# A two-layer mixture of experts behind a hybrid block: expert weights from the third expert on loaded in pieces of 1 MB in place of 2 MB

## The reference, cut to what matters

```
h = h + hybrid_mixer(rmsnorm_2(h, norm_mix[l]), w_in[l], w_branch_a[l], ...)
h = h + expert_choice_ffn(rmsnorm_2(h, norm_ffn[l]), w_router[l],
                          w_expert_gate[l], w_expert_up[l], w_expert_down[l])

# in expert_choice_ffn, cap = 2 * 256 // 16 = 32
gate, idx = lax.top_k(jnp.swapaxes(aff, 1, 2), cap)
xe = h[bidx, idx]
a = jnp.einsum('becd,edf->becf', xe, w_gate)
u = jnp.einsum('becd,edf->becf', xe, w_up)
ye = jnp.einsum('becf,efd->becd', jax.nn.silu(a) * u, w_down)
return jnp.zeros_like(h).at[bidx, idx].add(gate[..., None].astype(h.dtype) * ye)
```

## Time and profile before

| | us |
|---|---|
| runs | 1815.93, 1816.86, 1821.24 |
| median | 1816.86 |
| the profiled execution | 1824.18 |
| its span | 1822.4 |
| PE busy | 1546.2 (85%) |
| DVE busy | 761.6 (42%) |
| ACT busy | 596.6 (33%) |
| HBM read | 564.18 MB, 310 GB/s over the span |

### The profile page before, as it was taken

One profiled execution on the slowest core, in us unless ns is written; L12 is line 12 of the kernel. 1 busy time (PEld: TensorE's weight loads), 2 busy tenths in 40 slices (PEclk: granted clock), 3 DMA queues, 4 the chain that ended last, 5 costly groups with the idle time before them and its releaser, 6 DMA issues.

```text
span 1822.4 us, 34068 instructions
## 1 busy us (share of the span) xinstructions
PE 1546.2 (85%) x15300; PEld 1186.6 (65%) x15300; DVE 761.6 (42%) x1574; ACT 596.6 (33%) x1063; POOL 76.0 (4%) x87
## 2 busy tenths in 40 slices
PE   8999999999999999976666666999999966566665
PEld 7989998999799998533333333799896533233332
DVE  6896668887564665210110110536664201011011
ACT  5765646665455654000000000546642000000001
POOL 1020001000020101000000000001010000000000
PEclk9999999999999999998887877899999987888887
DMA  6443456555473559999999999853489999999997
GB/s 262 175 153 139 147 189 226 190 185 194 165 289 120 206 202 408 413 429 430 430 430 429 430 430 429 344 194 127 195 342 409 428 430 430 430 430 429 429 430 308
DMA packets 45841, 567.44 MB, mean 311 GB/s; under 512 B 6672, under 2 KB 7216, under 8 KB 10496
## 3 DMA queue, kind: packets, MB, share of 16 engines
q1 hardware_dynamic: 40176, 552.62, 73.9%
q0 software_dynamic: 3744, 12.03, 1.8%
q10 hardware_dynamic: 1776, 0.62, 0.1%
HBM read 564.18 MB, written 1.05 MB: 310 GB/s over the span
## 4 chain that ended last, share of the span: by engine, by line
PE 59%; DMA 35%; DVE 3%; another core or an unknown queue 2%; ACT 1%; issue 0%; SPq 0%; DVEq 0%; ACTq 0%
DMA slab<-in_slabs 34%; PE bank L587 14%; PE bank L588 14%; PE bank L589 14%; PE bank L1130 5%; PE bank L1182 2%; PE bank L944 1%; DMA sm<-in_fb 1%; PE bank L1003 1%; PE bank L1200 1%; PE bank L967 1%; PE bank L1107 1%; DVE wl L1222 1%; DVE xc L1345 0%; PE bank L550 0%
## 5 line engine op out<-in xcount | busy, mean ns | idle before, releaser
L1130 PE MATMUL bank<-slab,xe 128*32 128x256 f32 x4096 | 313.5, 462 | 160.2 <-DMA slab<-in_slabs 160.0
L1222 DVE TENSOR_TENSOR wl<-slab,wh 128x1024 fp32r<-128x1024 f32 (+1 forms) x286 | 348.0, 1230 | 186.5 <-ACT wh L1899 186.2
L587 PE MATMUL bank<-hth,wh 128*128 128x256 f32 x1344 | 388.0, 289 | 2.8 <-DVE wl L1222 2.7
L588 PE MATMUL bank<-htl,wh 128*128 128x256 f32 x1344 | 380.7, 283 | 0.0
L589 PE MATMUL bank<-hth,wl 128*128 128x256 f32 x1344 | 380.6, 283 | 0.0
L1899 ACT ACTIVATE wh<-slab 128x1024 fp32r<-128x1024 f32 (+1 forms) x286 | 296.2, 1046 | 169.0 <-PE bank L589 157.8
L1130 PEld LDWEIGHTS bank<-slab,xe 128*32 128x32 f32 x4096 | 142.8, 127 | 310.5 <-DMA slab<-in_slabs 204.2
L587 PEld LDWEIGHTS bank<-hth,wh 128*128 128x128 f32 x1344 | 257.8, 192 | 12.9 <-issue 7.8
L588 PEld LDWEIGHTS bank<-htl,wh 128*128 128x128 f32 x1344 | 257.9, 192 | 0.1
L589 PEld LDWEIGHTS bank<-hth,wl 128*128 128x128 f32 x1344 | 257.7, 192 | 0.0
L1182 PE MATMUL bank<-slab,ha 128*32 128x256 f32 x2048 | 142.7, 427 | 71.3 <-DMA slab<-in_slabs 69.7
(11 more groups left out here) (388 smaller groups left out, 2187.1 us busy)
## 6 DMA issues: line engine op xcount, KB each, us to landing
slab<-in_slabs SPq DMA_DIRECT2D x251, 2048.0 KB, 47.9
slab<-in_slabs SPq DMA_DIRECT2D x23, 1024.0 KB, 10.3
bias<-in_bias POOLq DMA_DIRECT2D x32, 192.0 KB, 3.1
bias<-in_bias POOLq DMA_DIRECT2D x8, 256.0 KB, 5.7
x<-in_x SPq DMA_DIRECT2D x2, 512.0 KB, 4.4
rg<-in_rg POOLq DMA_DIRECT2D x1, 1024.0 KB, 10.5
bt<-in_rel POOLq DMA_DIRECT2D x1, 768.0 KB, 14.6
fg<-in_final_g POOLq DMA_DIRECT2D x1, 512.0 KB, 4.0
```

What stands on the lines that cost most here:

```text
L587: e.matmul(o, wh, xh, start=start, stop=False, skip_group_check=True)
L588: e.matmul(o, wh, xl, start=False, stop=False, skip_group_check=True)
L1130: t = e.matmul(bk[bank][32 * j:32 * j + 32, 0:256], XE[:, c, :], w[:, k, 256 * j:256 * j + 256], start=(c == 0), stop=(c == 7))
L1222: e.tensor_tensor(lo, src, hi.bitcast(F32), ALU.subtract).then_inc(*dve_l.mark(p))
```

## The change

slab_list() names, for experts 3 to 15 of both layers, halves in place of whole slabs. "From the third expert on" counts from zero: experts 0, 1 and 2 keep their pieces. Each half has a load of its own with 1 MB (8 KB for each partition), a semaphore wait of TensorE ahead of its 16 matmuls and a mark behind them, and a slot of its own in slot_plan(). The order of the weights stays. tail_slab becomes the half (1, 0) of eg1_14, as the whole slab is no longer in the list, and the condition on the warming matmuls now names the last down slab of layer 0, so that they stand where they stood.

```diff
@@ slab_list
         for e in range(1, 16):
-            expert(f"eg{l}_{e}", [(0, 1), 1] if e == 2 else [0, 1], "late")
-            expert(f"eu{l}_{e}", [0, 1], "late")
-            expert(f"ed{l}_{e}", [0], "late")
+            both = [(0, 0), (0, 1), (1, 0), (1, 1)]
+            expert(f"eg{l}_{e}", [(0, 1), 1] if e == 2 else both if e > 2 else [0, 1], "late")
+            expert(f"eu{l}_{e}", both if e > 2 else [0, 1], "late")
+            expert(f"ed{l}_{e}", both[0:2] if e > 2 else [0], "late")
             if e == 1:
                 expert(f"eg{l}_2", [(0, 0)], "late")
-            expert(f"ed{l}_{e}", [(1, 0), (1, 1)] if e == 15 else [1], "late")
+            expert(f"ed{l}_{e}", both[2:4] if e > 2 else [1], "late")
@@ build
-    tail_slab = nslab["eg1_14", 1]
+    tail_slab = nslab["eg1_14", (1, 0)]
@@ tensor_program
                     for n, key, k0, nk in parts("ed", l, ex, i):
-                        if l == 0 and type(key) is tuple:
+                        if (l, ex, i) == (0, 15, 1) and type(key) is tuple:
                             warm(2, 5 if key[1] else 2)
```

## The result

| | before, us | changed, us |
|---|---|---|
| median of 9 runs each | 1816.68 | 1823.81 |
| range | 1814.68 to 1822.58 | 1821.98 to 1828.29 |
| ratio, with its 95% interval | | 1.0039 [1.0029, 1.0048] |
| profiled execution (span) | 1824.18 (1822.4) | 1825.38 (1823.5) |

The change costs 7.1 us, 0.39%. The forecast was +10.0 us. It is slower by more than the 0.3% that a measurement of this kernel tells from no change, though the interval reaches down to that.

The account below looks back on a forecast made before the run. The prediction took the expert stages to be bound by DMA, bytes over rate at 430 GB/s. +11.6 us for transfers, 0 for room and release and -1.6 at layer 0's end gave +10.0: 1826.9 us, range 1812.2 to 1833.8.

Parts of the forecast that it names:

- The toll of a transfer: Expert stages: 154 more transfers on the saturated queue, each costing 0.075 us beside its bytes, add 11.6 us.
- F: Cost of a load for being one transfer, beside its bytes; taken as 0.075 us, range 0.03 to 0.11.
- 10 us windows in the mixers: Start of each mixer: 1 MB loads at 421 and 422 GB/s against 429 for 2 MB loads, giving 0.099 us a transfer.
- the two landings at the end: Kernel's very end: two halves landed in 2.41 + 2.43 us against 4.86 for a whole load, giving -0.02 us a transfer.
- The rule that spoke against the change: Skill's 2.0 us fixed per transfer, as a toll +308 us; the prediction held it mostly hidden by other loads in flight.
- Room and release: Expert stages: half-slots, each half asked for once one half two experts earlier is used; a full queue hides it, 0 us.
- rival C of the prediction: Expert stages: the queue of ten transfers runs dry behind 12.8 us issue blocks, 19 us on top, 1846; chance 0.03.
- The end of layer 0: Layer 0's last expert: PE, not the last load, is late; halves start the last up-load's matmuls earlier, -1.6 us.
- The point named ahead as a check: Expert 15's up-load start less expert 9's: 180.3 us by the forecast, 177.6 if the toll is hidden, 174 if engines even out.
- A (hidden): Expert stages: the toll of a transfer is hidden, F from -0.02 to 0.03, 1812.2 to 1819.9 us; chance 0.30.
- B (evened engines): Expert stages: shorter transfers even the 16 engines out, each half landing at 2.42 us, -13.9 us, 1801; chance 0.07.
- D (PE the bound): Expert stages: PE at the low clock becomes the bound, at most +29 us less the DMA's 11.6, near 1845; chance 0.02.

Follow-up runs that it names:

- the two transfers alone: Kernel before with its slots, waits and releases, but each of the 154 slabs issued as two 1 MB transfers: 1823.98 us, ratio 1.0041.
- the second profile of before: The kernel before, unchanged, run and profiled once more: 1817.40 us, ratio 1.0005.
- the run with four transfers: Kernel before, but each of the 154 slabs issued as four 512 KB transfers with 4 KB rows: 1840.83 us, ratio 1.0131.
- the run for the last expert alone: The changed kernel's halves for expert 15 only, both layers; experts 3 to 14 keep 2 MB loads: 1817.58 us, ratio 1.0011 against the kernel before.

## Why the prediction was right, and where it was off

**The bound.** Right. The stages are bytes over rate; the rate fell by 1% and the kernel became 0.39% slower, with what PE, ScalarE and VectorE do nearly unchanged.

**The toll of a transfer, +11.6 us.** Right in its mechanism, and too large by half: the two transfers alone measured 7.7 us, so F is 7.7/154 = 0.050 us, where 0.075 was taken. By the rates it is 2.0972 MB at 426 GB/s less 2.0972 MB at 430, 4.923 - 4.877 = 0.046. The step that was mis-sized is the reading of 10 us windows in the mixers as if they were good to 1 GB/s. The burst of halves itself is the same in every kernel here, but comes at another time in each execution. By the first of its 8 KB packets it is in the changed kernel 3.7 us earlier in layer 0 and 2.5 in layer 1, in the second profile of before 6.0 and 9.5 us earlier. Windows that follow it read 423 and 424 in the changed kernel, and 427 and 418 in the second profile of before, where the first had 421 and 422:

```profile
508.30:518.30 10.00, 10.00 (x86) 10.00 (x85) 8.94 (x8) 5.66 (x8) 3.60 (x2) 1.00 1.00 423
1171.50:1181.50 10.00, 10.00 (x86) 10.00 (x85) 4.90 (x7) 5.98 (x8) 0.00 (x0) 1.00 1.01 424
```
```profile
506.00:516.00 10.00, 10.00 (x85) 10.00 (x85) 8.85 (x8) 6.24 (x8) 3.61 (x2) 1.00 1.01 427
1164.50:1174.50 10.00, 10.00 (x85) 10.00 (x85) 4.91 (x7) 5.90 (x8) 0.00 (x0) 1.00 0.99 418
670.00:680.00 10.00, 10.00 (x85) 10.00 (x85) 6.98 (x8) 3.81 (x5) 0.65 (x1) 1.00 1.02 436
```

(The last line is the window with 2 MB loads, 6 us earlier like the burst: 436, where the first profile had 429.) And in the first profile itself a window 1.0 or 1.5 us later reads 418 in place of 421 and 433 in place of 422:

```profile
513.00:523.00 10.00, 10.00 (x86) 10.00 (x85) 8.79 (x8) 5.47 (x7) 2.63 (x1) 1.00 1.01 418
1175.50:1185.50 10.00, 10.00 (x85) 10.00 (x85) 4.90 (x4) 4.73 (x6) 0.00 (x0) 1.00 1.04 433
```

So such a window is good to 5 or 10 GB/s, and F by the same formula is 0.03 us at 427 GB/s and 0.14 at 418. That the halves are slower than whole loads was read rightly; that the windows agreed within 1 GB/s was chance. The weighing with the two landings at the end, F = -0.02, pulled the term the right way, but that reading is no better: the same three landings of the second profile of before give 2.43 + 2.44 - 4.85 = +0.02. Neither reading alone would have given the time, +15.2 or -3.1 us for the term; the range of F taken around their mean, 0.03 to 0.11, holds the 0.050.

**The rule that spoke against the change.** A further transfer costs 0.014 to 0.017 us beside its rows, though a load lands 27 to 51 us after its issue. The Trainium skill's fixed 2.0 us for a transfer (DMA: Bandwidth & Descriptors, Anatomy of one DMA — SWDGE (gpsimd) path) would have made the change cost 308 us as a toll; the section states it for transfers that GpSimd issues, while the slabs go out on SP. The runs agree with the prediction that it is no toll in a full queue. Rows of 4 KB ran at 419 to 420 GB/s in the stages, and a set of 128 more rows costs 0.036 to 0.040 us. The estimate of 0.078 us, from the 408.7 GB/s that the same page gives for 4 KiB rows (iDMA fabric), is too large here.

**Room and release, 0 us.** Right. Two transfers without them took as long as the change within the intervals (-0.6 us). The queue in flight fell from 51 to 27 us, forecast was 25, and even 12.7 us in the run with four transfers left no dip: rival C of the prediction, the dry queue, has nothing for it, and its condition failed: the longest issue fell with the size of the load, from 12.8 to 6.65 us.

**The end of layer 0, -1.6 us.** Wrong. The step was to take the 12.1 us between the last up-load and the last matmuls for a property of the kernel. It was the clock of one execution (0.50 in both groups; 1.00 in the second in the repetition, and 9.88 us), and the run for the last expert alone shows no gain. What the change was to shorten is in most profiles bounded by the last load in either kernel, and a stretch seen in one profile was put at its full worth in the median. The rest of that step held: the third mixer load's later slot cost nothing, the stretch from the last matmuls of layer 0 to the first of layer 1's experts is 241.46 us where it was 241.45.

**The sum.** +11.6 - 1.6 = +10.0 against +7.7 (transfers alone) and +7.1 (all): the terms were off by -3.9 and by +1.6, and so partly made up for one another, which is luck. The point named ahead as a check, from expert 9's first up-load to expert 15's, is 1131.74 - 953.02 = 178.72 us after, 177.56 before; forecast were 180.3, and 177.6 if hidden. It lies in between, nearer to hidden, but the second profile of before has 1127.26 - 950.59 = 176.67: over 36 loads it was too short a piece to decide, as the steady 426 GB/s did.

**The rivals.** A (hidden) would have been 430 GB/s, B (evened engines) 433, and the forecast 423. The measured 426 refutes A and B, and the two transfers' interval of +5.3 to +9.6 us leaves out A's upper end, F = 0.03, as well. D (PE the bound) is refuted by PE's 67 to 69 us in 100.

## What to carry to other kernels

When a stretch is bound by its transfers, count rows and transfers besides bytes: here two transfers of 8 KB rows in place of one of 16 KB rows cost 0.05 us for each slab of 2 MB, and four of 4 KB rows 0.16, in a queue that was kept full. Finer waits and releases brought nothing here, where 10 loads were in flight. What splitting a last load wins where an engine waits for it, no run here shows; before splitting there look at a second profile, since the clock of one execution moved that place by 2 us, and a small load at the start moved the first expert by 6. Windows of 100 us in a steady stretch agreed within 2 GB/s between the two profiles of before; windows of 10 us read 418 to 433 GB/s for the same burst.

## What wasn't expected of the hardware

Transfers of 64 partitions, one for the lower and one for the upper half, 154 pairs of them, cost 455 us: 228 to 366 GB/s with a DMA share of 1.01, where 128 partitions had 430. The Trainium skill, SBUF — State Buffer, Can I just issue two DMAs to hit both halves?, says that the ports are picked by a single transfer's span of partitions, and that two concurrent transfers, at partition 0 and at partition 64, ran only 6% faster than one. The runs agree that two such halves don't make up one whole transfer: the lowest slice, 228 GB/s, is a little above half of 430. Why others reach 366 no run here shows.

What a queue holds is neither a fixed number of bytes nor of rows. In steady stretches the time from issue to landing, over the time between landings as an estimate of how many are in flight, was 51.2 us for loads of 2 MB and 128 rows (51.2/4.93 = 10 in flight), 27.1 for 1 MB and 128 rows (27.1/2.46 = 11), 12.7 for 512 KB and 128 rows (12.7/1.25 = 10), but 32.9 for 2 MB and 256 rows (7) and 23.8 for 2 MB and 512 rows (5):

```profile
DMA to landing us min/median/max: 31.7/32.9/37.6
```
```profile
DMA to landing us min/median/max: 22.8/23.8/28.7
```

(The one transfer of 8 KB rows, then of 4 KB rows, window 1000 to 1080 us.) In these runs it is ten or so transfers of 128 rows, and fewer of those with more rows, though not in proportion.
